# Eight-row final norm of a mixture-of-experts layer: residual rows loaded earlier, norms interleaved with the last two expert tiles, and a 0/1 product for shared rows

## What is computed

```python
aff = sigmoid(x @ router_w)                    # 16 experts in 4 groups
# best group, then the 2 best experts in it; gates = aff / sum of the two
h = silu(x @ w_gate[e]) * (x @ w_up[e]) * gate # 512 wide, for the tokens of expert e
ffn = sum over the 2 experts of h @ w_down[e]
x = layer_norm(ALPHA * x + ffn, ln2_g, ln2_b)  # ALPHA = 2 ** 0.25
```

## Time and profile before

| what | value |
|---|---|
| time, median of 3 runs (lowest to highest) | 978.63 us (976.64 to 979.17) |
| device time of the profiled execution | 974.39 us |
| its span | 972.6 us |
| TensorE busy | 895.8 us, 92% |
| VectorE, ScalarE, GpSimd busy | 681.0, 566.1, 345.5 us |
| mean granted TensorE clock | 0.975 |

### The profile page before, as it was taken

The page is one execution under the profiler, slowest core; times in us unless marked ns, Lnnn a source line. Parts: engine busy times, 40 slices in busy tenths (PEclk is TensorE's granted clock), DMA queues, the critical chain, the costliest instruction groups (busy, mean ns, idle before and its releaser), DMA issues.

```text
span 972.6 us, 16090 instructions
## 1 busy us (share of the span) xinstructions
PE 895.8 (92%) x4838; PEld 714.9 (74%) x4839; DVE 681.0 (70%) x1038; ACT 566.1 (58%) x818; POOL 345.5 (36%) x269
## 2 busy tenths in 40 slices
PE   7989999979989899999879999999999999999980
PEld 7867887845656558888657888888788788888760
DVE  5488899996889665466786648788888844225276
ACT  5376677787876767402444656787777735215342
POOL 0000059999999940000010212213323311111146
PEclk9999999999999999999989999999999999999995
DMA  8821022001001001535675889999999987552475
GB/s 230 205 70 42 24 67 88 1 1 23 1 1 45 2 11 36 172 108 195 272 256 196 272 299 325 403 388 397 404 389 394 366 307 244 142 148 65 100 245 209
DMA packets 64959, 173.63 MB, mean 179 GB/s; under 512 B 19809, under 2 KB 35169, under 8 KB 52592
## 3 DMA queue, kind: packets, MB, share of 16 engines
q1 hardware_dynamic: 56816, 144.13, 40.1%
q0 software_dynamic: 7616, 27.46, 11.4%
q10 hardware_dynamic: 480, 1.44, 0.5%
HBM read 142.79 MB, written 26.74 MB: 174 GB/s over the span
## 4 chain that ended last, share of the span: by engine, by line
PE 57%; DVE 18%; DMA 11%; issue 6%; ACT 6%; SPq 1%; DVEq 0%; ACTq 0%; POOLq 0%; POOL 0%
PE ps L484 14%; PE ps L486 14%; PE ps L485 14%; DMA raw<-in_w_gate 10%; DVE junk_dve L1586 6%; PE ps L880 3%; PE ps L850 3%; DVE wlo L1898 2%; DVE bias L1534 2%; PE ps L867 1%; PE ps L1025 1%; ACT whi L1354 1%; ACT junk_act L1191 1%; DVE sm L1739 1%; ACT probs L1262 1%
## 5 line engine op out<-in xcount | busy, mean ns | idle before, releaser
L1898 DVE TENSOR_TENSOR wlo<-raw,whi 128x2048 fp32r<-128x2048 f32 x94 | 211.8, 2288 | 52.5 <-ACT whi L1354 52.3
L1354 ACT CAST whi<-raw 128x2048 fp32r<-128x2048 f32 x96 | 180.4, 1911 | 48.3 <-DMA raw<-in_w_gate 18.8
L484 PE MATMUL ps<-whi,xgT_hi 128*128 128x512 f32 x384 | 153.1, 399 | 7.5 <-DVE xgT_lo L1908 5.5
L486 PE MATMUL ps<-whi,xgT_lo 128*128 128x512 f32 x384 | 151.0, 393 | 0.0
L485 PE MATMUL ps<-wlo,xgT_hi 128*128 128x512 f32 x384 | 150.9, 393 | 0.0
L484 PEld LDWEIGHTS ps<-whi,xgT_hi 128*128 128x128 f32 x384 | 73.1, 190 | 23.6 <-issue 9.1
L484 PE MATMUL ps<-xT_hi,w_hi 128*128 128x512 f32 (+1 forms) x232 | 88.7, 382 | 1.1 <-DVE w_lo L1471 1.1
L2120 POOL COPY idx_now<-slot_token 128x1 int32 (+1 forms) x24 | 8.8, 366 | 222.0 <-PE ps L1025 211.7
L485 PE MATMUL ps<-xT_lo,w_hi 128*128 128x512 f32 (+1 forms) x232 | 87.6, 378 | 0.0
L486 PE MATMUL ps<-xT_hi,w_lo 128*128 128x512 f32 (+1 forms) x232 | 87.6, 378 | 0.0
L486 PEld LDWEIGHTS ps<-whi,xgT_lo 128*128 128x128 f32 x384 | 72.9, 190 | 15.7
(11 more groups left out here) (351 smaller groups left out, 1915.6 us busy)
## 6 DMA issues: line engine op xcount, KB each, us to landing
raw<-in_w_gate SPq DMA_DIRECT2D x32, 1024.0 KB, 12.3
raw<-in_w_up SPq DMA_DIRECT2D x32, 1024.0 KB, 12.7
raw<-in_w_down SPq DMA_DIRECT2D x32, 1024.0 KB
w_raw<-in_w_in SPq DMA_DIRECT2D x14, 512.0 KB, 4.0
x_tok<-in_x SPq DMA_DIRECT2D x8, 512.0 KB, 7.7
wo_raw<-in_w_o SPq DMA_DIRECT2D x16, 256.0 KB, 3.0
x_res<-in_x SPq DMA_DIRECT2D x16, 256.0 KB, 3.4
x_d<-xa SPq DMA_DIRECT2D x4, 512.0 KB, 5.8
```

Source lines behind the costliest of these rows:

```text
L484: pe.matmul(out, l_hi, r_hi, start=start, stop=False)
L486: return pe.matmul(out, l_lo, r_hi, start=False, stop=stop)
L1354: act.copy(whi[:, n, :], raw[:, n, :]).then_inc(gu_hi if n < 4 else dn_hi, 1)
L1898: dve.tensor_tensor(wlo[:, n, :], raw[:, n, :], f32(whi[:, n, :]), ALU.subtract).then_inc(gu_lo if n < 4 else dn_lo, 1)
```

## The change

- **Rows three tiles ahead.** The eight row tiles, and `ln2_g` and `ln2_b` between them, are loaded by ScalarE's queue (`load_rows`), after the additions of tiles 0 to 20 have landed (`y_out` at `third_t * 16`) and ahead of `gated(prev_t)`. Row tiles 6 and 7 go where the raw weights of the last expert were. SyncE only stores.
- **Loops one tile shorter.** The loops of ScalarE and VectorE end after tile 21 and tile 22 is written out; TensorE's is unchanged. GpSimd's runs to `last_t` and `fetch(last_t + 1)` is written out.
- **Eleven norms.** Tile 21's tokens are now late too: n = 8 (`THIRD`) is a gathered tile, n = 9 (`PREV`) tile 22's, n = 10 (`LAST`) tile 23's. GpSimd adds the shift for n = 0 to 8, VectorE for the last two. There are three indirect stores.
- **Shared rows by a product.** Tile 22's result is no longer scattered into `acc_d`. It is added to the gathered rows in SBUF in two halves (`prev_added`), and for tokens that are in tiles 22 and 23 a 0/1 matrix `same_token` times tile 22's result starts the PSUM sum of `down(last_t)` (two float32 matmuls of 512 columns, `begun=True`). The comparisons of token lists are made from two small matmuls next to tile 0.
- **Norms among the last tiles.** Statistics, gain and reciprocal are separate helpers; four row tiles take the gain from SBUF, the others from PSUM. ScalarE makes the statistics of row tiles 4, 5 and 7 (`row_stats`, two activations with accumulation each).
- Semaphores are merged (`wpool_in` into `wu_in`; `fix_in` and `raw_logit` into `fix_set`), and each of the 16 expert counts is at least 1 tile, which with these inputs changes no number.

```diff
-            last_t = sp.value_load(last_tile, ...)
-            sp.wait_ge(gu_lo, last_load * 4 + 4)
-            sp.dma_start(ln2_g[:], ...) ; sp.dma_start(ln2_b[:], ...)
-            sp.wait_ge(y_out, prev_t * 16)
-            for t in range(NT):
-                sp.dma_start(x1_tile(t), acc_d[(t + 1) * P:(t + 2) * P, :]).then_inc(rows_at[t], 16)
...
@@ tensor
+            pe.wait_ge(both_in, 1)
+            for i in range(2):
+                last = pe.matmul(ps[:, 7, i * P:(i + 1) * P], token_f[:, i:i + 1].to_broadcast([P, P]), ident[:],
+                                 start=True, stop=True)
+            last.then_inc(both_mm, 1)
...
+            for c in range(2):
+                part = slice(c * 512, (c + 1) * 512)
+                pe.wait_ge(prev_added, c + 1)
+                if c:
+                    pe.wait_ge(y_set, last_t)
+                pe.matmul(pair(1)[:, part], same_token[:], ysb[:, part], start=True, stop=False)
+            down(last_t, loads(last_t), begun=True)
@@ scalar
+            def row_stats(n):
+                i = BY_SCALAR.index(n)
+                act.wait_ge(rows_at[n], 32)
+                if i:
+                    act.wait_ge(stat_act, 2 * i)
+                else:
+                    act.wait_ge(rows_at[7], 32)
+                act.activation(junk_rows[:], norm_rows(n), ACT.Identity, scale=1.0 / D, accum_out=mv2[:, n, 0:1]
+                               ).then_inc(stat_act, 1)
+                act.wait_ge(stat_act, 2 * i + 1)
+                act.activation(junk_rows[:], norm_rows(n), ACT.Square, scale=-1.0, bias=mv2[:, n, 0:1],
+                               accum_out=mv2[:, n, 1:2]).then_inc(stat_act, 1)
...
+            def load_rows():
+                last_load = act.value_load(expert_of[0:1, bass.ds(last_t, 1)], min_val=0, max_val=EXPERTS - 1)
+                act.wait_ge(x1_out, 16 * NT)
+                act.wait_ge(acc_out, 16 * NT)
+                act.wait_ge(y_out, third_t * 16)
+                for t in range(NT):
+                    if t == 6:
+                        act.wait_ge(gu_lo, last_load * 4 + 2)
+                    act.dma_start(norm_rows(t), acc_d[(t + 1) * P:(t + 2) * P, :]).then_inc(rows_at[t], 16)
+                    if t in (1, 3):
+                        act.dma_start((ln2_g if t == 1 else ln2_b)[:], ...).then_inc(ln2_in, 16)
...
+                with act.If(t <= third_t):
+                    tile(t, t - 1, t - 2, t + 1)
+                    gated(t)
+            tile(prev_t, third_t, fourth_t, prev_t + 1)
+            load_rows()
+            gated(prev_t)
             x_hi_part(last_t)
             split_new(last_t, [3], prev_t)
+            norm_sd(0)
             y_part(third_t)
             h_hi_part(prev_t)
+            norm_sd(1)
             split_new(prev_t, (4, 5), third_t)
+            norm_scale(0)
+            norm_scale(1)
+            row_stats(4)
+            norm_sd(2)
+            row_stats(5)
             gated(last_t)
             act.copy(pair(2), ln2_g[:]).then_inc(gain_set, 1)
+            norm_sd(3)
+            norm_sd(4)
+            norm_sd(5)
+            norm_scale(2)
+            act.wait_ge(dn_used, prev_t * 2 + 2)
+            act.wait_ge(y_out, prev_t * 16)
+            act.copy(ysb[:, 0:512], ps[:, 2, :]).then_inc(gain_set, 1)
+            act.copy(ysb[:, 512:], ps[:, 3, :]).then_inc(y_set, 1)
             h_hi_part(last_t)
...
@@ gpsimd
+            fetch(last_t + 1)
...
+            for t in range(NT):
+                pool.wait_ge(rows_at[t], 32)
+            add_rows(third_t)
+            pool.wait_ge(ln2_in, 32)
+            pool.wait_ge(y_out, prev_t * 16)
+            gather_rows(THIRD, idx_add)
+            pool.wait_ge(dn_lo, prev_load * 2 + 2)
+            add_b(0)
+            pool.wait_ge(idx_set, last_t + 2)
+            pool.wait_ge(xg_tr, last_t + 2)
+            gather_rows(PREV, idx_row[0])
+            pool.wait_ge(gu_used, last_t * 4 + 4)
+            gather_rows(LAST, idx_row[1])
+            for n in range(1, PREV):
                 add_b(n)
+            pool.wait_ge(both_in, 2)
+            pool.wait_ge(fin_done, PREV)
+            pool.wait_ge(out_done, 16 * NT)
+            store_rows(THIRD)
+            pool.wait_ge(both_in, 3)
+            store_rows(PREV)
+            pool.wait_ge(both_in, 4)
+            store_rows(LAST)
```

311 lines of the change are left out of this document (173 added, 138 removed).

## The result

The changed kernel takes 983.39 us (median of 14 runs, 978.40 to 985.47) beside 978.19 for the kernel before (14 runs, 971.39 to 980.17). The ratio is **1.0057, 95% interval 1.0038 to 1.0075**: slower by 3.7 to 7.3 us. The forecast was 976.0 with a range to 980.6, so it failed in sign and in size. The profiled execution has a span of 980.0 us and 981.76 us in all, against 972.6 and 974.39.

The account below looks back on a forecast made before the run. TensorE was busy 92% of the span, then idle for a 26.8 us tail set by GpSimd's additions and VectorE's norms. The largest of three chains gave -2.6 us: 978.63 to 976.0 us, range 973.0 to 980.6.

Parts of the forecast that it names:

- Shared port: VectorE instructions with two SBUF operands beside GpSimd's additions: taken as 0, at most 1.3 us on either engine.
- Loop ends: Nine empty iterations ahead of tile 22: 5.76 us on VectorE, 3.58 on ScalarE, TensorE waits 2.5; tile 23 starts 1.4 later.
- rival of tile 22 at half clock: TensorE's wait ahead of tile 22 halves its clock; all 48 matmuls doubled +10.9 us, median 985; slower case 0.10.
- Row loads: Ten transfers on ScalarE's queue after tile 20's scatter lands at 909.6; last row tile landed by 926.5 us.
- GpSimd's chain: Tile 21's scatter, gathers, additions 1 to 7 from 941.3 to 957.8, last store at 963.9; end 969.9 us.
- ScalarE's chain: Casts, scalings, four accumulating passes at 1.35 us, table loads; scaling 2 ends 942.1, 1.6 us of slack before addition 2.
- rival of dearer switches: Two table switches ahead of scaling 2 cost a further 1.4 us each: span 972.7, median 978.7, no change; chance 0.04.
- TensorE and VectorE: Tile 22's rows gathered by 943.6, tile 23's down product ends 952 to 954, VectorE reaches it 957.3, done 962.8.
- Head: Start of the experts: two float32 matmuls and five small VectorE instructions next to tile 0, taken as 0, at most 1 us.
- Sum: Three chains end within 1.1 us; span from 972.6 to 969.9, -2.7, taken as -2.6; median 976.0 us.

Follow-up runs that it names:

- e2_psum: Changed kernel with tile 22's shift copied to PSUM by ScalarE and read there by VectorE; also loops and token columns unaltered; ratio 1.0012 to the kernel before.
- c4_split: Changed kernel, loops two iterations shorter, token columns behind tile 1, tile 23's sum before tile 22's shift, tile 22's down-weight splits before norms; ratio 0.9976 to kernel before.
- c5_both: The kernel of c4_split with VectorE's split of the fourth piece of up weights also moved behind the token comparisons; ratio 0.9966 to the kernel before.
- b1_bounds: Kernel before with the loops of ScalarE and VectorE one empty iteration shorter; ratio 0.9996 to the kernel before.
- e1_bounds: Changed kernel with the loops of ScalarE and VectorE two empty iterations shorter; ratio 1.0020 to the kernel before.
- c1_psum: Changed kernel with loops two iterations shorter, token columns and their products behind tile 1's first steps, and tile 22's shift read from PSUM; ratio 1.0010 to kernel before.
- e5_late3: Changed kernel with VectorE's split of the fourth piece of up weights moved behind the token comparisons; ratio 1.0047 to the kernel before.
- e6_noprod: Changed kernel without the two float32 products that add tile 22's result to tokens shared with tile 23; ratio 1.0050 to the kernel before.

## Why the prediction was wrong

- **Shared port: the step that failed.** It was bounded by "0, and one gain and one shift waited out, 1.3 us" and taken at 0. Measured: 3.9 us on VectorE's shift, taken away by e2_psum with 3.5 us of tail, and 1.55 and 1.78 us at the two scatters. The bound had two faults. It let VectorE wait for one instruction of GpSimd, while it waited for the rest of one addition and all of the next. By the prediction's own times the shift starts at 956.0 and addition 7 runs until 957.8, so it would meet that one too, and not only `THIRD`. And it looked only at GpSimd's additions, not at its scatters, which the change moves beside splits. For the scatters the kernel before had the price in its own loop, where the prediction did not look:

```profile
682.73 2.28 DVE L1898 TENSOR_TENSOR wlo<-raw,whi 128x2048 fp32r<-128x2048 f32 x1
...
684.13 2.36 POOL L2135 DMA_INDIRECT acc_d<-ysb,idx_add  x1 [3.06 <-ACT ysb L1381]
...
884.13 1.61 POOL L2135 DMA_INDIRECT acc_d<-ysb,idx_add  x1 [5.10 <-ACT ysb L1381]
```

  A scatter that starts while a split runs took 2.23 to 2.36 us (six of them, 684 to 777 us), the others 1.59 to 1.63. The Trainium skill (SBUF — State Buffer, SBUF: two separate sides), the rule that spoke against the change, was right that the shift would wait; its "for the whole instruction" was too little beside GpSimd's queue of additions, and the upper bound taken from it, 1.3 us, was too low as well.
- **Loop ends: right in kind, nearly in size.** 5.15 us for 5.76 on VectorE (an iteration less is worth 0.70 in either kernel, but the ninth made the wait only 0.03 longer; what took the rest back stays open), 3.62 for 3.58 on ScalarE, 1.89 for 2.5 on TensorE. The rival of tile 22 at half clock came true in part: from 906.95 to 910.3 us the granted clock was at half, at 1.89 us of wait where I had thought 2.5 to be on the safe side. It cost TensorE 1.65 us, which by that rival's own reckoning (1.7 for the first 3.5) would be 0.8 at the end; the loads in ScalarE's queue covered it.
- **Row loads: late by their start.** Forecast, with 3.5 us added for start and middle, at 913.1 and 930.0; measured 914.40 and 932.2. The late start is the long scatter's (1.55 us), and the loads took 17.8 us for 16.9; ten issues took 5.5 us for 4.4, so tile 22's silu started at 920.08 and not 917.4, which nothing waited for long.
- **GpSimd's chain: right from addition 1 on.** Additions 1 to 8 took 18.65 us back to back for 18.85, the first store came 1.26 us behind the last of them. It is 3.3 us late by what stood ahead of it, the scatters above all.
- **ScalarE's chain: right.** The passes took 1.04 and 1.15 with reads of 0.18 that ran partly beside them, 1.2 each and so the lower bound and not the 1.35 taken; a table load costs 1.28 with nothing behind it (944.70, the root at 946.00), so the rival of dearer switches falls.
- **TensorE and VectorE: the gather was mis-sized.** It was given 4.7 us to land and took 5.78, and it started 3.5 us late with the rest of GpSimd's chain; TensorE waited 7.10 us instead of about 5. VectorE's queue covered it while the long step stood behind.
- **Head: 0 taken, 1 as bound; 0.8 measured there, 0.4 at tile 22.** The change also puts VectorE's five small instructions ahead of tile 0's hidden rows, for which TensorE waits.
- **Sum.** 2.6 us of gain were forecast, 4.6 of loss came: 7.2 off. 3.5 of them are the long step (e2_psum), 3.3 the two scatters (1.55 and 1.78 by their lengths), 0.7 the middle, of which 0.4 is the head: 7.5, with a small gain left elsewhere. The scatters' share is by their lengths only: taken away one at a time they gave 0.5 and 0.2 us of tail, and 1.7 and 1.0 in c4_split and c5_both. c5_both, which has next to nothing of the long step, the long scatters and the head (its shift still took 1.85 us and its gather of tile 21's rows 1.40), ends at -2.6 in middle and tail; I estimate 0.7 to 1.4 of it from the shorter loops (b1_bounds has 0.7 for one iteration). So the rest of the sum was right to 0.7 to 1.4 us, and that c5_both ends where the forecast was is in part luck.

## What to carry to other kernels

When a change moves work of GpSimd in time, its indirect DMAs included, list which of VectorE's instructions with both operands in SBUF then stand beside it, and price each meeting by a row: for GpSimd the rest of the one that runs, for VectorE the rest of GpSimd's whole queue; look in the loop, where some iterations meet and some do not. An operand in PSUM, or the other order, frees such an instruction at little cost. Where several collisions stand in series, a fix shows its worth only when those behind it are gone too, so judge it by its local rows and not by its span alone.

## What the runs showed of the hardware

- A queue of GpSimd's additions kept VectorE out until it was empty: VectorE's shift, ready at 962.70 us while the second of three additions ran, got in at about 966.6 (its end less 1.28), behind the third; in e1_bounds it was ready at 956.48 during the first of three, took 6.34 us, and the third ended at 961.73. With one addition in the queue it was one: a gain that starts with addition 0 in e1_bounds (937.49 us) took 3.48 us instead of 1.28.
- The other way round GpSimd waited only for VectorE's instruction that was running, and got in between two splits, whose length did not change (3.70 us beside 4.50 of splits). Where the running split had 0.88, 1.67, 1.89 and 2.22 us left (684.13 in the kernel before, both scatters of the changed one, c1_psum), the scatter was 0.76, 1.55, 1.78 and 2.10 us longer than 1.60: the rest of the split less 0.1 each time. The copy of 128 integers in e5_late3 (2.04 us for 0.18) fits this too.
- VectorE's TENSOR_TENSOR with both inputs in SBUF delays GpSimd's indirect DMA: 1.60 us alone, 2.2 to 3.7 beside it, and 2.28 instead of 1.00 for a gather in the loop. A gain with both inputs in SBUF (SCALAR_TENSOR_TENSOR) does so too: 1.99 for 1.00 in e6_noprod. The Trainium skill (SBUF — State Buffer, Who interferes with whom) infers that a TENSOR_TENSOR leaves the writing of descriptors alone; here the issue as a whole was held. It also reads its column of indices from SBUF, and no run parts that from the writing of descriptors. The scatter of e1_bounds, recorded 0.03 us behind a split's start and not delayed, may have been first: the two splits took 4.56 us there and not 4.50. That is not shown.
- TensorE's granted clock fell to half (1.2 GHz) 3 us after a wait of 1.89 us had begun, and stayed there for 3.4 us; waits of 1.17 and 1.76 us in the kernel before and of 0.49 in e1_bounds left it at 1.00.
